# The second block's mixer rebuilt: z by tokens last, values first, the delta rule of four heads in 29 slot-wide steps, norms folded in as logs

## The reference, cut to what matters

```python
h = rmsnorm_2(x, norm_g); proj = h @ w_in            # 2048 -> q,k,v,z | b,a | q,k,v of attention
qkv_a = silu(causal_dwconv_2(qkv_a, gdn_conv_w))     # 4 taps
beta = sigmoid(b_a); g = -exp(a_log) * softplus(a_a + dt_bias)
o_a = gated_delta_rule(l2norm(q_a), l2norm(k_a), v_a, g, beta)   # chunks of 64 tokens
o_a = rmsnorm_2(o_a, gdn_norm_g) * silu(z_a)
o_b = rmsnorm_2(moba_attention(q_b, k_b, v_b, rel_bias), moba_norm_g)
x = x + concat(o_a, o_b) @ w_out
```

## Time and profile before

| | before |
|---|---|
| median of 3 runs | 2694.04 us (2693.04 to 2694.52) |
| profiled execution, its own time | 2691.33 us |
| its span | 2690.0 us |
| TensorE busy (matmul / weight load) | 2556.1 us, 95% / 2467.1 us, 92% |
| VectorE, ScalarE, GpSimd busy | 1624.9, 1041.7, 237.7 us |
| mean granted TensorE clock | 0.97 of 2.4 GHz |
| chain of work that ended last | PE 88%, DVE 7%, ACT 3% |
| mixer, first to last slot | about 1135 to 1826 us |

### The profile page before, as it was taken

How to read it: one execution, slowest core, us unless ns; L and a number is a source line. 1 busy time by engine, 2 the same in 40 slices (tenths; PEclk the granted TensorE clock), 3 DMA queues, 4 the chain that set the end, 5 groups by cost and what they waited for, 6 DMA issues and landing times.

```text
span 2690.0 us, 44604 instructions
## 1 busy us (share of the span) xinstructions
PE 2556.1 (95%) x19320; PEld 2467.1 (92%) x19320; DVE 1624.9 (60%) x2036; ACT 1041.7 (39%) x1186; POOL 237.7 (9%) x116
## 2 busy tenths in 40 slices
PE   8999999999999999989899788698899999999997
PEld 7888799999999999988898687597899999999997
DVE  5998675554555555766747324454766665666666
ACT  3000644444344444435336223443443433433433
POOL 0000000000000000033423322130000000000000
PEclk9999999999999999979999888898999999999998
DMA  7445555555655655434334223243455555555553
GB/s 231 149 145 171 178 186 182 190 184 174 188 188 181 182 186 181 153 116 135 103 102 144 75 80 118 93 141 110 150 185 182 181 181 181 188 187 181 181 187 118
DMA packets 244483, 428.55 MB, mean 159 GB/s; under 512 B 16408, under 2 KB 57664, under 8 KB 244288
## 3 DMA queue, kind: packets, MB, share of 16 engines
q1 hardware_dynamic: 240208, 422.63, 49.1%
q10 hardware_dynamic: 4080, 3.07, 0.4%
HBM read 423.54 MB, written 3.67 MB: 159 GB/s over the span
## 4 chain that ended last, share of the span: by engine, by line
PE 88%; DVE 7%; ACT 3%; issue 2%; DMA 1%; POOL 0%; ACTq 0%; DVEq 0%; SPq 0%
PE product L468 71%; PE product L493 9%; DVE squares L1364 2%; DVE w_lo L427 1%; PE small L1431 1%; PE small L1238 1%; ACT w_hi L420 1%; PE small L1447 1%; PE product L490 1%; PE small L1441 1%; PE small L1716 0%; DVE delta_work L1614 0%; PE small L1498 0%; DVE partial_sum L562 0%; PE small L1497 0%
## 5 line engine op out<-in xcount | busy, mean ns | idle before, releaser
L427 DVE TENSOR_TENSOR w_lo<-w_raw,w_hi 128x1024 fp32r<-128x1024 f32 x640 | 793.1, 1248 | 685.7 <-ACT w_hi L420 684.3
L420 ACT ACTIVATE w_hi<-w_raw 128x1024 fp32r<-128x1024 f32 x712 | 746.6, 1058 | 1056.7 <-PE product L468 1047.7
L468 PE MATMUL product<-h_hi,w_hi 128*128 128x256 f32 x2816 | 815.6, 290 | 12.5 <-DVE h_lo L534 10.6
L468 PE MATMUL product<-h_lo,w_hi 128*128 128x256 f32 x2816 | 803.4, 285 | 0.0
L468 PE MATMUL product<-h_hi,w_lo 128*128 128x256 f32 x2816 | 803.0, 285 | 0.0
L468 PEld LDWEIGHTS product<-h_hi,w_hi 128*128 128x128 f32 x2816 | 547.7, 195 | 20.6 <-issue 8.2
L468 PEld LDWEIGHTS product<-h_lo,w_hi 128*128 128x128 f32 x2816 | 547.7, 194 | 3.5 <-issue 3.4
L468 PEld LDWEIGHTS product<-h_hi,w_lo 128*128 128x128 f32 x2816 | 547.1, 194 | 0.0
L468 PE MATMUL product<-mid_hi,w_hi 128*128 128x256 f32 x1472 | 418.0, 284 | 7.0 <-DVE w_lo L427 5.3
L468 PE MATMUL product<-mid_lo,w_hi 128*128 128x256 f32 x1472 | 417.3, 283 | 0.0
L468 PE MATMUL product<-mid_hi,w_lo 128*128 128x256 f32 x1472 | 417.2, 283 | 0.0
(11 more groups left out here) (265 smaller groups left out, 2316.5 us busy)
## 6 DMA issues: line engine op xcount, KB each, us to landing
w_raw<-in_mlp_w SPq DMA_DIRECT2D x256, 512.0 KB, 3.7
w_raw<-in_w_in SPq DMA_DIRECT2D x112, 512.0 KB, 3.6
w_raw<-in_w_gate SPq DMA_DIRECT2D x88, 512.0 KB, 3.6
w_raw<-in_w_up SPq DMA_DIRECT2D x88, 512.0 KB, 3.5
w_raw<-in_w_down SPq DMA_DIRECT2D x88, 512.0 KB, 3.6
w_raw<-in_cc_w_in SPq DMA_DIRECT2D x128, 256.0 KB, 2.9
w_raw<-in_cc_w_out SPq DMA_DIRECT2D x32, 512.0 KB, 4.6
w_raw<-in_w_out SPq DMA_DIRECT2D x32, 512.0 KB, 3.7
```

The lines of the kernel that those rows point to most:

```text
L420: act.activation(k.w_hi[i % SPLIT], k.w_raw[i % RAW], ACT.Copy).then_inc(*k.act_done.mark("w_hi", i))
L427: dve.tensor_tensor(k.w_lo[i % SPLIT], k.w_raw[i % RAW], k.w_hi[i % SPLIT].bitcast(F32), ALU.subtract).then_inc(*k.dve_done.mark("w_lo", i))
L468: done = pe.matmul(out, stationary, moving, start=first and opens, stop=final, skip_group_check=True)
```

## The change

Everything around the mixer's slots is written anew; the slots themselves, their number and the split products stay.

- Order of slots: q, k, v of both groups (0 to 47), attention values (`moba` 4 and 5, 48 to 63), attention q and k (64 to 95), z by tokens (96 to 111), then `w_out` with the attention half first.
- The gates: the weights of b and a become the stationary operand, 48 matmuls stream 256 tokens; two transposes bring the rows back.
- Norms of q and k: squares by ones of one column (32 multiplications for both groups), ln and exp on `[128, 8]` tiles; the k norm goes into the exponent of the decay, the rest into factors. No tile is normed.
- The delta output is made by tokens: `inter` (q by state) and `intra` in multiplications of 128 columns; its norm is a factor per token, and z gates it there; it is turned back by TensorE.
- A group takes 29 steps, not 41 (the constant `DELTA_STEPS` = 28 paces GpSimd). GpSimd masks level n two or three steps ahead of `y`.
- Attention: probabilities aren't divided by their sum, the norm that follows takes it in. Heads 4 to 7 begin at step 97. The bias is fetched from ScalarE's queue, not SP's.
- Norms of x everywhere: ScalarE writes the high part of gain times x itself, VectorE the low part in one pass; squares are added as whole tiles, folded once at the end.

```diff
-MOBA_BLOCKS = [0, 2, 4, 1, 3, 5]
-W_OUT_ORDER = [(0, 0), (0, 1), (1, 0), (1, 1), (0, 2), (1, 2), (0, 3), (1, 3)]
+MOBA_BLOCKS = [4, 5, 0, 2, 1, 3]
+W_OUT_ORDER = [(1, 0), (1, 1), (0, 0), (0, 1), (1, 2), (0, 2), (1, 3), (0, 3)]
...
-def dve_squares(k, dve, name, g, which=0, before=None):
-        dve.tensor_reduce(k.partial, tiles, AX.X, ALU.add).then_inc(*k.dve_done.mark())
-        dve.tensor_tensor(out, out, k.partial, ALU.add).then_inc(*k.dve_done.mark("sums", name, g))
+def dve_squares(k, dve, name, g, into=0):
+        dve.tensor_tensor(out, out, k.sq.at(name, g).rearrange("p k t -> p (k t)"), ALU.add).then_inc(
+            *k.dve_done.mark("square sum", name, g))
+    if g == CT - 1:
+        for n in (2 * T, T):
+            dve.wait_ge(*k.dve_done.last())
+            dve.tensor_tensor(out[:, 0:n], out[:, 0:n], out[:, n:2 * n], ALU.add).then_inc(*k.dve_done.mark("sums", name))
...
+def act_prepare(k, act, norm, b, x, target_free, made, gain):
+    for n in range(b * CT, (b + 1) * CT):
+        done = act.activation(x.hi[:, n, :], k.x[:, n, :], ACT.Copy, scale=gain_column(k, gain, n))
+def dve_prepare(k, dve, norm, b, gain, x):
+    for n in range(b * CT, (b + 1) * CT):
+        done = dve.scalar_tensor_tensor(out=x.lo[:, n, :], in0=k.x[:, n, :], scalar=gain_column(k, gain, n),
+                                        in1=x.hi[:, n, :].bitcast(F32), op0=ALU.mult, op1=ALU.subtract)
...
+    for kt in range(KT):
+        wide = slice(kt * n, kt * n + P)
+        for j, (w, x) in enumerate([(k.w_ba_hi, k.h.hi), (k.w_ba_hi, k.h.lo), (k.w_ba_lo, k.h.hi)]):
+            done = pe.matmul(bank[:, 0:T], w[:, wide], x[:, kt, :], start=kt == 0 and j == 0, stop=kt == KT - 1 and j == 2)
...
+    yield
+    bank = open_bank("sums of squares", g)
+                done = pe.matmul(bank[:, i:i + 1], k.qk_squares[n][:, h, cut(t)], k.m("ones")[:, 0:1], start=True, stop=True)
+    done.then_inc(*k.pe_done.mark("sums of squares", g))
+    yield
+    for t in range(TT):
+        bank = open_bank("rows", g, t)
+        pe.wait_ge(*k.dve_done.at("logs by column", g, t))
...
+    act.activation(k.logs[:, 1, :, hs], logs[1], ACT.Ln, bias=k.eps[:, 0:1]).then_inc(*k.act_done.mark("logs", g))
+    act.activation(k.unit[:, :, :, hs], k.logs[:, :, :, hs], ACT.Exp, scale=-0.5).then_inc(*k.act_done.mark("unit", g))
...
 def pool_delta(k, pool, g):
-    yield from idle(5 + TT + 5 + TT + TT + 1)
-    for n in range(2, 7):
+    yield from idle(6)
+    for n in LEVELS:
...
+    k.act_beside.finish()
+    act.wait_ge(*k.pe_done.at("w_in", 3, 1))
+    for g in range(2):
+        act_part(k, act, k.h, 2 + g, CT, k.mk[g], k.act_done.at("moba norm", g), "heads_out")
```

More of the change, by code:

```diff
@@ L357, in plan @@
         for g in range(2):
-            for part in range(4):
+            for part in range(3):
                 product(("w_in", part, g), "w_in_2", part * GW + g * COLS, 2)
@@ L535, in dve_part, with act_squares @@
         *k.dve_done.mark("lo", name, g))
[L538 to L541, removed]
+def act_squares(k, act, name, g, src, made, gain=None, into=0):
+    if g:
+        sq, free = k.sq.take(name, g)
+        for f in free:
+            act.wait_ge(*f)
+    else:
+        sq = k.tmp_buf[into]
     act.wait_ge(*made)
@@ L1331, in pe_column_sums @@
-def pe_column_sums(k, pe, name, g, n_before, n_after):
-    flat = k.sq.at(name, g).rearrange("p k t -> p (k t)")
-    yield from idle(n_before)
-    for half in range(2):
-        bank, free = k.bank.take(name, g, half)
-        for f in free:
-            pe.wait_ge(*f)
-        pe.wait_ge(*k.act_done.at("squares", name, g))
-        pe.matmul(bank, k.m("ones"), flat[:, half * 512:(half + 1) * 512], start=True, stop=True).then_inc(
-            *k.pe_done.mark(name, g, half))
-        yield
-    yield from idle(n_after)
@@ new lines, in pool_delta @@
+def pool_delta(k, pool, g):
+    yield from idle(6)
+    for n in LEVELS:
+        for t in range(TT):
+            pool.wait_ge(*k.act_done.at("a turned", g, t))
+            if n > 2:
+                pool.wait_ge(*k.pe_done.at("y", g, n - 1, t))
+            elif g:
+                pool.wait_ge(*k.pe_done.at("y", 0, 6, t))
+            pool.tensor_tensor(k.off[t], k.a_t[t], four(k.m(f"merge{n}_t")), ALU.mult).then_inc(*k.pool_done.mark("off", g, n, t))
+        yield
+        yield
+    yield from idle(DELTA_STEPS - 16)
@@ new lines, in pe_turn, with act_turned @@
+def pe_turn(k, pe, name, g, src, ready):
+    for half in range(2):
+        bank, free = k.bank.take(name, g, half)
+        for f in free:
+            pe.wait_ge(*f)
+        pe.wait_ge(*ready)
+        for n in range(CT):
+            h, t = half * 2 + n // TT, n % TT
+            done = pe.transpose(bank[:, cut(n)], src(t, h), k.m("identity"))
+        done.then_inc(*k.pe_done.mark(name, g, half))
+def act_turned(k, act, name, g, out, gain):
+    for half in range(2):
+        act.wait_ge(*k.pe_done.at(name, g, half))
+        act.activation(out[:, half * 2:half * 2 + 2, :], k.bank.at(name, g, half).rearrange("p (h t) -> p h t", h=2), ACT.Copy,
+                       scale=k.col(gain, 0)).then_inc(*k.act_done.mark(name, g))
+        k.bank.give((name, g, half), k.act_done)
```

1426 lines of the change are left out of this document (791 added, 635 removed).

## The result

| | before | after |
|---|---|---|
| median, runs timed side by side | 2693.66 us (4 runs) | 2580.43 us (4 runs, 2578.66 to 2583.70) |
| ratio to before | | 0.9581, 95% interval 0.9564 to 0.9597 |
| profiled execution, span | 2690.0 us | 2578.6 us |
| VectorE, ScalarE busy | 1624.9, 1041.7 us | 1527.1, 1066.4 us |

The forecast was 2577, between 2555 and 2620. To see where the 111.4 us of the two spans went, I first count what TensorE lost. The busy time by stretch of the changed kernel: from the norm of x to the entry of `w_out`, then the norm ahead of the last part, then pieces of the first.

A forecast was written before the change was run, and what follows sets the result against it. TensorE was taken as the bound, losing idle time and half clock in the mixer's stretches. Savings summed to 117 us, from 2691.3 to 2574; with 2.7 for the median, 2577 us, range 2555 to 2620 (8 in 10).

The forecast's parts named there:

- start of the mixer: 1124 to 1184 us: whole-tile adds replace ten strided reduces and VectorE's scaling pass goes; saves 9 of 15.2 us (5 to 15).
- gates: 1184 to 1205 us: 48 multiplications of 256 columns replace 96 of 16, taking 5.8 us; saves 15 us (12 to 17).
- delta rule: 1205 to 1500 us: 16 reciprocals go, three new waits come; saves 17 of 32.1 us (−3 to 28).
- levels: Group 1, 1500 to 1590 us: GpSimd masks three steps ahead of `y`, its wait goes; saves 32 of 33.6 us (10 to 34).
- attention, entry, `finish()`: 1590 to 1750 us: attention and entry to `w_out` net 0 (−15 to 10); `finish()` saves 26 us (20 to 27).
- TensorE's own work beyond the gates: Column sums save 10 us, delta outputs 10, new one-column sums cost 7; together 13 us saved (5 to 18).
- last norm, with cross attention's heads: 1876 to 1926 us, norm ahead of the last part: four reduces become adds; saves 5 of 11.0 us (2 to 9).
- Rival A: Group 1's levels: GpSimd still releases late, so 22 to 25 of the 32 us stay; 2600 us, chance 0.07.
- The new waits: Delta groups: 3.2 us at each of two log steps, 4.2 at group 0's masks, 3.4 more for half clock.
- Table loads: Eight loads in TensorE's chains at 1.28 us each; the skill's added drain would cost 11 us more, 2588, weight 0.05.
- Rival B: New in-order waits in some ten steps and a doubled `w_out` entry cost: some 33 us more, 2610 us, chance 0.22.
- C: Mixer's 112 slots: ScalarE becomes the bound, needing 4.8 us per slot; slower, above 2699 us, chance 0.03.

## Why the prediction was right

The n-th `w_hi` belongs to the same slot position in both traces, so the lead of the changed kernel at its start is the saving so far: −0.6 us at the 277th, 6.9 at the 301st (1166.7 before, 1159.8 after), 25.4 at the 309th (1216.3 and 1191.0), 105.9 at the 417th (1772.5 and 1666.6), 105.3 at the 441st and 111.5 at the 461st and the last. The 80.5 between the 309th and the 417th split as follows: idle and half clock were 62.3 in the two delta groups (1216 to 1590) and are 20.3 (1191 to 1490); from there on they were 45.2 and are 22.3; the rest, 15.6, is work.

| term | predicted | measured |
|---|---|---|
| start of the mixer | 9 | 7.5 |
| gates | 15 | 18.5 |
| delta rule and levels | 17 + 32 | 42.0 |
| attention, entry, `finish()` | 0 + 26 | 22.9 |
| TensorE's own work beyond the gates | 13 | 15.6 |
| first blocks; rest of `w_out` and products for cross attention | 0 | −1.2 |
| last norm, with cross attention's heads | 5 | 6.2 |
| sum | 117 | 111.5 |

The sum is 5.5 off while single terms are up to 7 off in both directions, so some of its closeness is luck: the gates and TensorE's own work gave 6.1 more than I took, the delta rule with its levels and the entry 10.1 less. The profiled execution took 2580.0 us for the 2574 of my sum; the median stood 0.5 above it, not 2.7, which made the miss of the median smaller, 3.4 us. The last row moves by 2 us with the half clock at cross attention's heads, as shown above, which no term of mine had.

*Start and last norm.* The mechanism holds: putting the strided reduces back costs 6.1 at either place, 12.2 of the 13.7 that the two terms gave. Of the two waits I kept, that on GpSimd's first `w_lo` is there (2.6); that on the two-pass norm, which I kept at 2.8, fell to 0.6.

*Gates.* 48 in 5.7 us for 5.8. The saving is 3.5 above mine, about the wait of 3.3 ahead of them. My bound that had this wait in it was added up wrongly: 15 and 3.3 give 18, not 17, so the measured 18.5 lies outside it.

*Levels.* The best supported step: late masking brings the waits back (31 us), early masking in the old kernel takes 22.6 off, 26.4 by the medians. Rival A is refuted.

*Delta rule.* Together with the levels 42 for 49, and the reason for the first part holds only in part. Half of the 7 is in the count (62.3 us were lost there, where my two stretches had 65.7), half is 3.6 us more of waits and half clock left over than I expected. I put most of the 32 lost down to the reciprocals; without them the old kernel saves 14 there. The new waits came as sized at the masks (4.6 + 0.6 for 4.2), and smaller at the logs: 2.8 and 1.0 for 3.2 each, the 2.8 in this one profile only. Not foreseen were group 1's waits at its first `y` (1.2 + 2.5) and the half clock behind the sums.

*Entry.* I expected about 8 us in line and 2.5 + 1.7 at the norms; TensorE waited 3.1 + 4.8 + 3.1 at the entry and 2.7 at the first norm. The 7.1 for the bias and `finish()` went. But I put the 7.1 down to the bias's queue alone, and without the reciprocals it fell to 2.2 with the bias still in SP's queue. What the move did by itself wasn't run.

*Own work.* The column sums of q and k cost 3.7 and 3.5 us, 7.2 for the predicted 7. The delta outputs take 6.2 + 4.4 us busy for 10 to 12, 12 less than before.

*Table loads.* The two loads between sums and rows in the changed kernel:

```profile
1216.54 1.28 ACT L1629 ACT_TABLE_LOAD   x1
1217.83 0.27 ACT L1629 ACTIVATE logs<-small,epsilons 128x8 f32<-128x8 f32 x1
1218.00 0.26 ACT L1630 ACTIVATE logs<-small,epsilons 128x8 f32<-128x8 f32 x1
1218.28 1.28 ACT L1633 ACT_TABLE_LOAD   x1
1219.57 0.22 ACT L1633 ACTIVATE unit<-logs 128x16 f32<-128x16 f32 x1
```

The activation starts 0.01 us after the load's end. The drain of the Trainium skill, "ScalarE: Activation LUTs", section "What ACT_TABLE_LOAD costs", isn't seen on the path, and the 11 us that it would have added didn't come. Nor did the same page's section "Table sets: the hidden batching unit" hold for this program: exp behind ln loads a second time.

Rival B did not come as a whole, but its mechanism lives in group 0's masks and at the entry. C is far off: ScalarE is busy 25 us more over the whole program, which is 0.2 us a slot if all of it is put on the mixer's 112. VectorE is busy 98 us less, where I expected some 80.

## What to carry to other kernels

Where engines keep their order, a queue's length matters only in the step in which another engine waits: two operations of 1.24 us cost 4.9 us a level behind a `w_lo`, and nothing two or three steps sooner. Removing one wait often showed the next in line: VectorE's masks behind GpSimd's, k turned behind VectorE's. And edits that gave 2 to 8 us each stood too near to the spread of one kernel's runs (up to 6 us) to be judged alone; together they gave 23. Last, count a multiplication with 1 or 16 columns as one with 256.

## What the runs showed of the hardware

- Narrow multiplications take the clock down with no idle time ahead or between. 96 of 16 columns ran gapless, 43 records of that stretch at clock 1.00 and the rest at 0.51. 32 records of one column, also gapless, were followed by a slot at 0.63; in two lots of 16 by one at 1.00.
- GpSimd and VectorE hold each other up. A VectorE operation on two SBUF tiles that takes 0.69 us alone took 2.71 beside GpSimd's `w_lo`, and 0.69 when that `w_lo` was gone. The Trainium skill, "GPSIMD Engine Reference", section "8. Key points", says that GpSimd shares its SBUF interfaces with VectorE's two-input instructions; the trace agrees, and shows which one is held: the one that starts second. In the changed kernel all 40 VectorE operations with two SBUF inputs that began inside a two-input operation of GpSimd ended behind it, by about 0.3 us with 256 columns, 0.55 with 512 and 1.1 with 1024. Where VectorE's began first, GpSimd's grew instead: a `w_lo` of 2.4 us alone took up to 3.1 behind one VectorE operation of 1.22 (1667.77 us). A VectorE operation with an input in PSUM runs beside a `w_lo` unhindered, as here (`small` is PSUM):

```profile
1407.60 0.69 DVE L1789 TENSOR_TENSOR delta_work<-delta_work,small 128x512 f32<-128x512 f32 x1 [0.20 <-PE small L1543]
1407.01 2.36 POOL L435 TENSOR_TENSOR w_lo<-w_raw,w_hi 128x1024 fp32r<-128x1024 f32 x1 [2.38 <-ACT w_hi L420]
```

  In the kernel before 42 of 50 ended behind. The other eight began within 0.3 us of GpSimd's start, or in a row directly behind one that had; they kept their usual length, and GpSimd's `w_lo` beside them took 2.7 to 5.3 us.
- Up to 256 columns a column costs nothing here: records with 1, 16 and 256 columns started 0.11, 0.11 and 0.12 us apart at full clock (a float32 multiplication of one column has two records, the others one).
